# Building the expert pairs' scatter matrices inside each pair's turn, with a re-ordered last pair and filler products at the rank step

## The reference, cut to what matters

```python
def hierarchical_moe(h, w_rg, b_rg, w_re, b_re, w_g, w_u, w_d):
    ...
    group_probs = jax.nn.softmax((t @ w_rg + b_rg).astype(jnp.float32), axis=-1)
    p_group, g_idx = lax.top_k(group_probs, 1)
    ...
    p_exp, e_idx = lax.top_k(jax.nn.softmax(in_group, axis=-1), TOP_K)
    weights = p_group * p_exp / jnp.sum(p_exp, axis=-1, keepdims=True)
    ...
        act = jax.nn.silu(jnp.einsum("td,edh->teh", t, w_g[sl])) * jnp.einsum("td,edh->teh", t, w_u[sl])
        out = out + jnp.einsum("teh,ehd->td", act * combine[:, sl, None], w_d[sl])
```

## Time and profile before

| | us |
|---|---|
| median of 3 runs | 1789.89 (1787.4 to 1792.51) |
| profiled execution, its own time | 1785.16 |
| its span | 1783.5 |
| PE busy | 1688.9 (95%) |
| DVE busy | 942.7 (53%) |
| ACT busy | 623.9 (35%) |
| mean granted TensorE clock | 0.955 |

### The profile page before, as it was taken

One profiled execution on the slowest core, in us unless ns is written; L12 is line 12 of the kernel. 1 busy time (PEld: TensorE's weight loads), 2 busy tenths in 40 slices (PEclk: granted clock), 3 DMA queues, 4 the chain that ended last, 5 costly groups with the idle time before them and its releaser, 6 DMA issues.

```text
span 1783.5 us, 29470 instructions
## 1 busy us (share of the span) xinstructions
PE 1688.9 (95%) x11249; PEld 1332.3 (75%) x11249; DVE 942.7 (53%) x1630; ACT 623.9 (35%) x1032; POOL 3.7 (0%) x9
## 2 busy tenths in 40 slices
PE   9999999899889999999989899999999898999997
PEld 8999999899779989998979644444379885444444
DVE  6888876833545688887896401111169753111112
ACT  5544465223455444344315221111151442111112
POOL 0000000000000000000000000000000000000000
PEclk8999998997999999998999889999989997999998
DMA  8998634214233568884335379999924453999993
GB/s 333 358 353 306 251 131 153 71 48 166 83 119 131 213 233 309 306 305 167 120 118 185 151 276 368 377 361 372 372 95 143 159 206 129 367 368 362 375 367 129
DMA packets 115795, 420.79 MB, mean 236 GB/s; under 512 B 12944, under 2 KB 13088, under 8 KB 115568
## 3 DMA queue, kind: packets, MB, share of 16 engines
q1 hardware_dynamic: 114624, 414.19, 64.1%
q0 software_dynamic: 1072, 5.21, 0.8%
HBM read 416.73 MB, written 2.62 MB: 235 GB/s over the span
## 4 chain that ended last, share of the span: by engine, by line
PE 76%; DVE 14%; ACT 5%; issue 4%; DMA 0%; DVEq 0%; SPq 0%; ACTq 0%
PE work L842 19%; PE work L1465 12%; PE acc L842 10%; PE work L1489 7%; DVE yconv L2494 5%; PE work L1412 5%; PE work L934 5%; PE acc L1499 4%; PE work L802 2%; DVE wlo L1966 2%; PE work L877 2%; ACT whi L1523 2%; PE work L919 1%; PE work L812 1%; DVE yslo L2722 1%
## 5 line engine op out<-in xcount | busy, mean ns | idle before, releaser
L1966 DVE TENSOR_TENSOR wlo<-raw,whi 128x1024 fp32r<-128x1024 f32 x264 | 321.3, 1223 | 189.2 <-ACT whi L1523 188.8
L1523 ACT ACTIVATE whi<-raw 128x1024 fp32r<-128x1024 f32 x264 | 277.0, 1056 | 283.5 <-PE work L842 189.0
L842 PE MATMUL work<-hhi,whi 128*128 128x256 f32 x1024 | 294.2, 287 | 1.7 <-DVE hlo L1994 0.8
L842 PE MATMUL work<-hlo,whi 128*128 128x256 f32 x1024 | 292.5, 286 | 0.0
L842 PE MATMUL work<-hhi,wlo 128*128 128x256 f32 x1024 | 292.3, 285 | 0.0
L842 PEld LDWEIGHTS work<-hhi,whi 128*128 128x128 f32 x1024 | 199.0, 194 | 3.8 <-DVE wlo L1966 2.5
L842 PEld LDWEIGHTS work<-hlo,whi 128*128 128x128 f32 x1024 | 199.1, 194 | 0.2
L842 PEld LDWEIGHTS work<-hhi,wlo 128*128 128x128 f32 x1024 | 198.9, 194 | 0.0
L2709 DVE COPY xg<-work 128x256 f32<-128x256 f32 x28 | 11.9, 425 | 301.3 <-PE work L1412 301.3
L1465 PE MATMUL work<-over_splits,xg 128*64 128x512 f32 x480 | 126.2, 622 | 4.7 <-ACT xg L1926 3.4
L2072 DVE SCALAR_TENSOR_TENSOR ada_tiles<-ada_tiles,c_act 128x1024 f32<-128x1024 f32 x96 | 116.2, 1218 | 1.4 <-DMA ada_tiles<-ada_d 1.4
(11 more groups left out here) (423 smaller groups left out, 3052.1 us busy)
## 6 DMA issues: line engine op xcount, KB each, us to landing
raw<-wstream_d SPq DMA_DIRECT2D x448, 512.0 KB, 4.8
over_splits<-wstream_d SPq DMA_DIRECT2D x192, 512.0 KB, 5.6
ada_tiles<-ada_d SPq DMA_DIRECT2D x96, 512.0 KB, 5.3
over_pool<-wstream_d SPq DMA_DIRECT2D x48, 512.0 KB, 5.6
bias_rows_d<-rt POOLq DMA_DIRECT2D x1, 1536.0 KB, 11.0
xT<-x_d SPq DMA_DIRECT2D x4, 256.0 KB, 3.8
mem_in<-mem_d POOLq DMA_DIRECT2D x1, 1024.0 KB, 5.2
tb<-bias_rows_d POOLq DMA_DIRECT2D x1, 1024.0 KB, 7.7
```

The costliest lines, as they stand in the source:

```text
L842: mm = pe.matmul(out, a, b, start=(start and k == 0), stop=(stop and k == n - 1), skip_group_check=skip)
L1523: act.activation(whi[n % AHEAD][:], tiles[SLOT[SPLITS[n]]][:], ACT.Copy).then_inc(s("hi_done"), 1)
L1966: dve.tensor_tensor(wlo[n % AHEAD][:], tiles[SLOT[SPLITS[n]]][:], whi[n % AHEAD][:].bitcast(F32), ALU.subtract).then_inc(s("lo_done"), 1)
```

## The change

There are three parts. `W` is gone and `V` is now one event of each of the 16 turns, after gu 2: two transposing products, two four-column products into the same PSUM bank 1, a 128x256 ACT copy, and two small DVE reductions that wait for this copy. `G` k=0 waits for both and now stands behind d k=0. With it the loop over turns 2 to 13 is gone; all 16 turns are written out. In the tail the last pair's work goes by halves, and `Y` is two events, one for each half. Thirteen dummy products are issued before PE waits for the mask.

```diff
-def moe_events(eng, event):
+def moe_events(event):
...
-    def turn(p, i):
+    def turn(p):
         d, scatter, gather = p >= 1, p >= 2, p // 2 + 1 < FOURS
-        event("gu", p, 0, i)
+        event("gu", p, 0)
         if p == 0:
-            event("rest", 0, 1, i)
-        elif p == 1:
-            event("W", 0, 0, i)
-        event("gu", p, 1, i)
-        if p < 2:
-            event("V", p, 0, i)
+            event("rest", 0, 1)
+        event("gu", p, 1)
         if d:
-            event("T", p - 1, 0, i)
+            event("T", p - 1, 0)
         if scatter:
-            event("S", p - 2, 0, i)
-        event("gu", p, 2, i)
+            event("S", p - 2, 0)
+        event("gu", p, 2)
         if p == 0:
-            event("rest", 0, 2, i)
-        if p < 2:
-            event("V", p, 1, i)
-        event("gu", p, 3, i)
+            event("rest", 0, 2)
+        event("V", p, 0)
+        event("gu", p, 3)
+        if d:
+            event("d", p - 1, 0)
         if gather:
-            event("G", p, 0, i)
-        if p == 0:
-            event("V", p, 2, i)
+            event("G", p, 0)
+        event("gu", p, 4)
+        if gather:
+            event("G", p, 1)
         if d:
-            event("d", p - 1, 0, i)
...
         if d:
-            event("Y", p - 1, 0, i)
+            event("Y", p - 1, 0)
+            event("Y", p - 1, 1)
     for c in range(DC):
-        event("first", 0, c, None)
-    event("rest", 0, 0, None)
-    turn(0, None)
-    turn(1, None)
-    with eng.Fori(0, (PAIRS - 4) // 4) as i:
-        for p in range(2, 6):
-            turn(p, i)
-    turn(PAIRS - 2, None)
-    turn(PAIRS - 1, None)
-    event("T", PAIRS - 1, 0, None)
+        event("first", 0, c)
+    event("rest", 0, 0)
+    for p in range(PAIRS):
+        turn(p)
+    event("T", PAIRS - 1, 0)
+    event("d", PAIRS - 1, 0)
+    event("d", PAIRS - 1, 1)
+    event("S", PAIRS - 2, 0)
+    event("S", PAIRS - 2, 1)
+    event("Y", PAIRS - 1, 0)
+    event("S", PAIRS - 2, 2)
+    event("d", PAIRS - 1, 2)
+    event("d", PAIRS - 1, 3)
+    event("Y", PAIRS - 1, 1)
     for j in range(3):
-        event("S", PAIRS - 2, j, None)
-    for j in range(4):
-        event("d", PAIRS - 1, j, None)
-    event("Y", PAIRS - 1, 0, None)
-    for j in range(3):
-        event("S", PAIRS - 1, j, None)
+        event("S", PAIRS - 1, j)
+S_LAST = [(PAIRS - 2, DC // 2 - 1)] + [(PAIRS - 1, m) for m in (1, 3, 5)]
...
+                hold(1, 13)
                 pe.wait_ge(s("mask_ready"), l + 1)
...
-                    elif what == "W":
-                        pe.wait_ge(s("selectT_ready"), 8 * l + 5)
-                        for n in range(PAIRS):
-                            for q in range(QT):
-                                mm = pe.matmul(work[2][:, 4 * n:4 * n + 4], select[:, q, n, :], halves[:, q, n, :],
-                                               start=(q == 0), stop=(q == QT - 1))
-                        mm.then_inc(s("wslot_mm"), 1)
                     elif what == "V":
...
+                        if p == 0:
+                            pe.wait_ge(s("g_copy"), G_DVE_ALL * l + DC // 2)
+                            pe.wait_ge(s("slots_ready"), 4 * l + 2)
+                        else:
+                            pe.wait_ge(s("act_turned"), base + p)
+                        if p == 1:
+                            pe.wait_ge(s("slots_ready"), 4 * (l + 1))
+                        for q in range(QT):
+                            pe.matmul(work[1][:, q * P:(q + 1) * P], select[:, q, p, :], identr[:],
+                                      start=True, stop=True)
+                        for q in range(QT):
+                            mm = pe.matmul(work[1][:, T:T + 4], select[:, q, p, :], halves[:, q, p, :],
+                                           start=(q == 0), stop=(q == QT - 1))
                         mm.then_inc(s("selectT_mm"), 1)
                     elif what == "G":
+                        if k == 0:
+                            pe.wait_ge(s("selectT_ready"), base + p + 1)
+                            pe.wait_ge(s("wslot_read"), 2 * (base + p + 1))
...
                     elif what == "d":
                         if k == 0:
-                            pe.wait_ge(s("act_turned"), along(base + p + 1, i, 4))
-                            if p >= 1:
-                                pe.wait_ge(s("y_low"), along(2 * (base + p), i, 8))
-                            else:
-                                pe.wait_ge(s("selectT_ready"), 8 * (l + 1))
+                            pe.wait_ge(s("act_turned"), base + p + 1)
+                        if p >= 1 and k % 2 == 0:
+                            pe.wait_ge(s("y_low"), 2 * (base + p) - 1 + k // 2)
...
                     elif what == "S":
                         if k == 0:
-                            pe.wait_ge(s("y_low"), along(2 * (base + p) + 2, i, 8))
+                            pe.wait_ge(s("y_low"), 2 * (base + p) + (1 if p == PAIRS - 1 else 2))
...
                         for m in range(*S_PART[k]):
+                            if p == PAIRS - 1 and m == DC // 2:
+                                pe.wait_ge(s("y_low"), 2 * (base + p) + 2)
...
-                            if p == PAIRS - 1 and m in (1, 3, 5):
+                            if (p, m) in S_LAST:
                                 mm.then_inc(s("s_last"), 1)
...
                     elif what == "V":
-                        r = 6 * p + k
-                        act.wait_ge(s("selectT_mm"), 8 * l + r + 1)
-                        act.activation(selectT[:, 2 * r:2 * r + 2, :].rearrange("p c t -> p (c t)"),
-                                       work[2 + r % 2][:, :], ACT.Copy).then_inc(s("selectT_ready"), 1)
+                        act.wait_ge(s("selectT_mm"), base + p + 1)
+                        act.activation(selectT[:, p, :], work[1][:, 0:T], ACT.Copy).then_inc(s("selectT_ready"), 1)
...
                     elif what == "Y":
-                        act.wait_ge(s("pe_tile"), along(moe_tile(l, "d", p, 3) + 1, i, MOE_TURN))
-                        if p > 0:
-                            act.wait_ge(s("s_mm"), along(base + p, i, 4))
+                        act.wait_ge(s("pe_tile"), moe_tile(l, "d", p, 2 * k + 1) + 1)
+                        if p == 0:
+                            act.wait_ge(s("wslot_read"), 2 * (base + 1))
+                        elif p == PAIRS - 1 and k == 0:
+                            act.wait_ge(s("s_last"), len(S_LAST) * l + 1)
                         else:
-                            act.wait_ge(s("wslot_read"), 2 * (l + 1))
...
+                            act.wait_ge(s("s_mm"), base + p)
...
-                    elif what == "W":
-                        dve.wait_ge(s("wslot_mm"), l + 1)
+                    elif what == "V":
+                        dve.wait_ge(s("selectT_mm"), base + p + 1)
+                        dve.wait_ge(s("selectT_ready"), base + p + 1)
                         for j in range(2):
                             rows = slice(64 * j, 64 * j + 64)
-                            dve.tensor_reduce(rt[rows, 576:576 + PAIRS],
-                                              spread(work[2][rows, j:j + 1], (PAIRS, 2), (4, 2)), X_AXIS, ALU.add
+                            dve.tensor_reduce(rt[rows, 576 + p:577 + p], spread(work[1][rows, T + j:T + j + 1], (2,), (2,)), X_AXIS, ALU.add
                                               ).then_inc(s("wslot_read"), 1)
```

More of the change, by code:

```diff
@@ L141, in turn @@
+        event("gu", p, 4)
+        if gather:
+            event("G", p, 1)
         if d:
-            event("d", p - 1, 0, i)
-        event("gu", p, 4, i)
-        if p == 0:
-            event("V", p, 3, i)
+            event("d", p - 1, 1)
+        event("gu", p, 5)
+        if scatter:
+            event("S", p - 2, 1)
+        event("gu", p, 6)
         if gather:
-            event("G", p, 1, i)
+            event("G", p, 2)
+        if scatter:
+            event("S", p - 2, 2)
         if d:
-            event("d", p - 1, 1, i)
@@ L150, in turn @@
[L150 to L157, removed]
+            event("d", p - 1, 2)
+        event("gu", p, 7)
+        event("A", p, 0)
+        if d:
+            event("d", p - 1, 3)
         if gather:
-            event("G", p, 2, i)
-        if scatter:
-            event("S", p - 2, 2, i)
+            event("G", p, 3)
@@ L1414, in gather, with event @@
                     mm.then_inc(s("g_mm"), 1)
-                def event(what, p, k, i):
+                def event(what, p, k):
                     if what == "first":
@@ L1928, in event @@
                     elif what == "A":
[L1929 removed]
+                        act.wait_ge(s("pe_tile"), moe_tile(l, "gu", p, 7) + 1)
                         act.activation(pair_a[:, 0, :], work[0][:, 0:T], ACT.Silu).then_inc(s("msilu"), 1)
                     elif what == "T":
[L1932 removed]
+                        act.wait_ge(s("turn_mm"), base + p + 1)
```

(25 more changed lines are left out.)

73 lines of the change are left out of this document (21 added, 52 removed).

## The result

The changed kernel takes 1778.0 us (median of 6, 1775.7 to 1778.3) against 1790.0 for the kernel before; ratio 0.993, with a 95% interval of 0.992 to 0.994 (so for the ratios below). That is 12 us, 0.7%, faster; forecast were 7.9 us (1782.0, range 1776 to 1790).

What follows compares the result with a forecast made beforehand. PE (TensorE) was taken to bound the kernel, its work in a turn being time. Terms summed to -4.9 us in layer 0 and -3.0 in layer 1, together -7.9: median 1782.0 us, 0.44% faster, range 1776 to 1790.

Steps and rivals of the forecast that it cites:

- Turn 1, -9.3 and -7.8: Turn 1 of layers 0 and 1 shortens to 15.3 us; 4.6 us each from W and V's, the rest slow clock.
- Turn 0, -2.6: Turn 0 of each layer: six V's go, one comes, G 0 waits 0.3 us more; net -2.6 us.
- Turns 2 to 15, +10.4: In each layer 14 new V's at 0.74 us, hidden by nothing, add 10.4 us.
- loop, -0.9: Writing the loop over turns out removes three loop boundaries, -0.9 us in each layer.
- V's chain is hidden: In each turn V's copy, reductions and hand-overs make 1.0 us; gu 3 and d 0 give 1.9 before G 0.
- slower rival: V's chain ahead of G 0 makes PE wait 0.5 us in each of 28 turns, +14 us: 1796; chance 0.08.
- Tail, -2.4: Last pair's work by halves lets the residual start at 1300.35 in place of 1302.77: -2.4 us in each layer.
- Dummies, -0.1 and +0.3: At the rank step, 13 dummy products change layer 0 by -0.1 us and layer 1 by +0.3.
- dummy rival: Either of two: dummies at half clock, +3.3 to +7 us, chance 0.08; or they keep the gathers warm, 1776.8 us, 0.08.
- The clock rival: The 7.9 us of slow clock in turn 1 don't come back or are lost elsewhere: 1789.9, no change; chance 0.24.

Runs made afterwards that it cites:

- run 1: Kernel before with turns 2 to 13 written out and nothing else: 1786.9 us, ratio 0.998.
- run 2: Changed kernel without the 13 dummy products: 1779.6 us, ratio 0.9945.
- run 3: Changed kernel with the last pair's tail in the old order: 1782.3 us, ratio 0.996.
- run 4: Kernel before with the loop written out, the new tail and the dummies, V and W as before: 1779.9 us, ratio 0.994.
- run 8: Changed kernel with V's two transposing products issued twice, six products in a V: 1787.0 us in a single execution.
- run 7: Changed kernel with 14 more dummy products behind the clear of acc, ahead of the flag: 1774.2 us, ratio 0.990.
- run 5: Changed kernel with V of turns 2 to 15 directly behind S 0, ahead of gu 2: 1767.3 us, ratio 0.987.
- run 10: Changed kernel with V behind S 0 in turns 2 to 15, 14 dummies behind the clear, S 1 directly behind G 1: 1756.0 us, ratio 0.979.

## Why the prediction was right, point by point

- *The whole.* The range held and the mechanism of each part was right, but the sum was too small: 12.0 us came where 7.9 were forecast, most of the difference from turns 2 to 15. By parts the forecast had the tail at 4.8 us, the loop at 1.8, V's and W's move at 1.5 (22.3 gained in turns 0 and 1, 20.8 spent in turns 2 to 15) and the dummies at -0.2. Runs 1 to 4 have 4.3 for the tail, 2.8 for the loop, 1.9 for the move and at most 1.6 for the dummies, the last two within overlapping intervals; 1.4 us of the 12 are in none of them.
- *Turn 1, -9.3 and -7.8.* Right: 15.3 us was forecast and measured in both layers, and no fall of the clock. Right for this trace, though: with W the clock was at the lower level for 3.4 to 10.2 us by layer and execution (before, runs 1 and 4), half of which is lost time by the estimate in run 4. I had given that weight only in the rival. So it is partly luck that the move's net came near the sum's: without falls of that length it would have been a loss.
- *Turn 0, -2.6.* Measured -3.1 in both layers.
- *Turns 2 to 15, +10.4, and loop, -0.9.* The largest miss. A V costs 0.69 (run 4), not 0.74, which makes +9.7; and writing the loop out gives -2.2 (run 1), not -0.9. I had counted boundaries only; the trace had the rest: `yslo` waits of 2.8 us in twelve turns, of which 1.2 were the loop's own, and 0.9 of the 3.7 for ACT's copy. Together +7.3 and +7.2 were measured against +9.5 a layer: 4.6 us of the 5.3 that the segments are better than forecast. The figure of the Trainium skill, "TensorE: Matmul & The Clock Gate", section "Back-to-back issue gap", about 81 ns a product, gave the estimate of 0.59 for a V; the traces don't agree with it: a product measured 0.113 us (run 8).
- *V's chain is hidden* behind gu 3 and d 0: right, PE's waits in turns 2 to 13 are 4.4 us with V (changed kernel) and without it (run 4). The slower rival is out.
- *Tail, -2.4.* Measured -2.67 and -2.56; in the median 4.3 of the 4.8 forecast arrive (run 3). S's first half and Y's first half overlap as worked out. That the residual's 3.43 us on DVE bound what follows was wrong for layer 0: there the norm's products wait for ACT, which rounds weights first (run 3).
- *Dummies, -0.1 and +0.3.* Measured -0.34 and +0.19 against before, -0.45 and -0.13 against run 2, which has all else of the change, and of that 0.2 in all is left at the first gu. The gathers stayed at 1.2 GHz as said; neither dummy rival came true, but a second set of dummies did what the first couldn't (run 7).
- *The clock rival* (time lost elsewhere) came partly true in the profiled pair: of 13.2 us gained in the expert stages 6.4 went in stages that are the same. The medians don't show it, 12.0 against 13.2, so it is a matter of single executions.

## What to carry to other kernels

Count the changes between weight shapes on a bound matrix engine, not only its products: here a block of full-width products between half-width ones cost 0.32 to 0.35 us for standing alone, and putting such blocks side by side brought 10.7 and 8.0 us (9.0 and 8.5 by the segments), where the re-cut of V and W had brought at most 1.9. A fall of the clock is worth taking out, but price it by several executions, since its length moved by a factor of three. Fill a pause that comes just ahead of dense work with dummies, not one that is followed by another pause.

## What the runs showed of the hardware

- At full clock a product with its own 128-column weight load costs 0.113 us at 128 columns (run 8) and 0.12 at four.
- A block of such products between products with 64-column weights costs 0.32 us (V, run 5) or 0.35 (S 1, run 10) more than one beside others of its kind.
- With waits and addresses by a loop's register DVE started 0.1 us later in a turn's last step, and twelve turns took 2.2 us more than written out (run 1). The written-out turns ran beside 357 to 376 GB/s of weights, and PE's only waits in turns 2 to 13 were 4.4 us for ACT and DVE.
- PE reads the flag and takes the branch while 14 products are still being worked off: in layer 1 it is 4.7 us from their start to the first gather, where the products alone take 3.2 and the pause without them was 3.8 (run 7).
- The time of unchanged stages differs by up to 8 us between the profiled executions of these kernels (997.2 to 1005.1 ahead of layer 0's router), not all of it in step with the time at 1.2 GHz (88.7 for 997.2, 1004.6 and 1005.1). What the rest is stays open.
